# Mixture of experts: gate and up as seven half-size products in the two column halves of the array

## What is computed

```python
def route_set(hs):
    aff = jax.nn.softmax((hs @ w_router + b_router).astype(jnp.float32), axis=-1)
    gate, idx = lax.top_k(aff.T, cap)
    xe = hs[idx]
    hid = jax.nn.silu(jnp.einsum('ecd,edf->ecf', xe, w_gate)) * jnp.einsum('ecd,edf->ecf', xe, w_up)
    ye = jnp.einsum('ecf,efd->ecd', hid, w_down) * gate[..., None].astype(hid.dtype)
    return jnp.zeros(hs.shape, ye.dtype).at[idx.reshape(-1)].add(ye.reshape(-1, hs.shape[-1]))
```

## Time and profile before

| | |
|---|---|
| median of 3 runs | 4300.24 us (4299.25 to 4301.16) |
| profiled execution: span | 4305.1 us |
| PE busy | 3853.5 us, 90% of the span |
| DVE, ACT, POOL busy | 1393.0, 844.8, 419.3 us |
| bytes by DMA | 612.73 MB, mean 142 GB/s |
| experts of layer 0, layer 1 | from 1427 to 2324 us, from 3594 to 4296 us |

### The profile page before, as it was taken

How to read it: one execution, slowest core, us unless ns; L and a number is a source line. 1 busy time by engine, 2 the same in 40 slices (tenths; PEclk the granted TensorE clock), 3 DMA queues, 4 the chain that set the end, 5 groups by cost and what they waited for, 6 DMA issues and landing times. The chain is left out here.

```text
span 4305.1 us, 59887 instructions
## 1 busy us (share of the span) xinstructions
PE 3853.5 (90%) x25486; PEld 2161.3 (50%) x25486; DVE 1393.0 (32%) x2991; ACT 844.8 (20%) x1952; POOL 419.3 (10%) x675
## 2 busy tenths in 40 slices
PE   6899999677897799999997899998697886999998
PEld 4565445476644344444443655444486542444444
DVE  2452112687634200000002453113778443101010
ACT  3342010544311000000002342011534210000000
POOL 1100000221200000000001100000232100000000
PEclk9999999788998899999998899999698997999999
DMA  6201110200174666666663001110100328888884
GB/s 230 108 1 30 56 52 1 76 13 18 65 280 192 239 250 245 244 248 249 245 239 113 24 6 30 58 45 28 58 10 12 114 91 313 304 322 303 322 302 157
DMA packets 190041, 612.73 MB, mean 142 GB/s; under 512 B 34473, under 2 KB 42921, under 8 KB 183121
## 3 DMA queue, kind: packets, MB, share of 16 engines
q1 hardware_dynamic: 169232, 542.30, 33.6%
q0 software_dynamic: 20544, 66.60, 5.2%
HBM read 561.07 MB, written 47.79 MB: 141 GB/s over the span
## 5 line engine op out<-in xcount | busy, mean ns | idle before, releaser
L2534 PE MATMUL ps<-moe_w,e_hT 128*128 128x512 f32 x1024 | 445.9, 593 | 6.1 <-ACT e_hT L2578 6.1
L2497 PE MATMUL ps<-moe_w,e_xT 128*128 128x512 f32 x1024 | 450.5, 598 | 0.8 <-ACT e_xT L2559 0.8
L2504 PE MATMUL ps<-moe_w,e_xT 128*128 128x512 f32 x1024 | 444.7, 592 | 0.0
L529 PE MATMUL ps<-hT,p_w 128*128 128x512 f32 (+1 forms) x880 | 327.1, 534 | 0.0
L2497 PEld LDWEIGHTS ps<-moe_w,e_xT 128*128 128x128 f32 x1024 | 194.7, 192 | 246.7 <-issue 245.5
L2504 PEld LDWEIGHTS ps<-moe_w,e_xT 128*128 128x128 f32 x1024 | 194.6, 190 | 244.9 <-issue 244.9
L2600 DVE TENSOR_TENSOR e_hid<-e_hid,ps 128x512 f32<-128x512 f32 x64 | 43.9, 687 | 837.9 <-PE ps L2504 837.9
L2534 PEld LDWEIGHTS ps<-moe_w,e_hT 128*128 128x128 f32 x1024 | 192.0, 190 | 239.0 <-issue 239.0
L2181 PE MATMUL ps<-M,yT 128*128 128x512 f32 x576 | 259.8, 606 | 11.1 <-DMA o_br<-in_b_router_dram 7.6
L529 PEld LDWEIGHTS ps<-hT,p_w 128*128 128x128 f32 x880 | 167.2, 190 | 159.3 <-issue 153.1
L1021 PE MATMUL ps<-M 96*128 96x512 f32 (+1 forms) x400 | 183.2, 544 | 2.9 <-PEq L727 2.1
(11 more groups left out here) (356 smaller groups left out, 5507.2 us busy)
## 6 DMA issues: line engine op xcount, KB each, us to landing
moe_w<-in_w_gate_dram SPq DMA_DIRECT2D x64, 2048.0 KB, 13.2
moe_w<-in_w_up_dram SPq DMA_DIRECT2D x64, 2048.0 KB, 10.7
moe_w<-in_w_down_dram SPq DMA_DIRECT2D x64, 2048.0 KB, 17.0
o_mod_w<-in_w_ada_dram SPq DMA_DIRECT2D x24, 1024.0 KB, 10.9
m_mod_w<-in_w_ada_dram SPq DMA_DIRECT2D x16, 1024.0 KB, 5.8
p_w<-in_w_in_dram SPq DMA_DIRECT2D x6, 2048.0 KB, 7.9
r_z<-z_rows SPq DMA_DIRECT2D x20, 512.0 KB, 3.3
z_rows<-p_zo POOLq DMA_DIRECT2D x36, 256.0 KB, 2.3
```

What stands on the lines that cost most here:

```text
L529: ins = nc.tensor.matmul(ps[:, j % NB, 0:tw], w[n % RW][:, k, m * P:(m + 1) * P], hT[:, k, t0:t0 + tw], start=(k == 0), stop=(k == KT - 1))
L2497: ins = nc.tensor.matmul(ps[:, c, :], xT[:, 4 * half + k], wp[:, k, c * 512:(c + 1) * 512], start=(half == 0 and k == 0), stop=(half == 1 ...
L2504: ins = nc.tensor.matmul(ps[:, 2 + c, :], xT[:, 4 * half + k], wp[:, k, c * 512:(c + 1) * 512], start=(half == 0 and k == 0), stop=(half = ...
L2534: ins = nc.tensor.matmul(ps[:, 6 + c, :], hT2[:, 4 * half + k], wp[:, k, c * 512:(c + 1) * 512], start=(half == 0 and k == 0), stop=(half ...
```

## The change

Gate and up, seen as two matrices, are each a product of 128 tokens by 1024 by 1024. Both are cut in two along tokens, contraction and columns, and the eight block products are replaced by seven products of sums and differences of blocks (Winograd's form of Strassen's scheme). One product is 64 tokens by 512 by 512 for gate and for up at once: gate in array columns 0 to 63 (PSUM partitions 0 to 63) and up in columns 64 to 127, `ps[HF * q:HF * q + HF, b]`, 16 recorded matmuls of 64 stationary columns. DVE now forms four token sums (128 by 256 elements) and eight weight sums (128 by 2048 elements) an expert, the latter in place in the weight slots or in `t2`. ACT copies the growing sum in bank A three times an expert (`partial`), DVE joins four outputs from it (`joined`), and since up's outputs land in the other partitions, ACT moves them across after silu. Two of an expert's products, P1 and P2, and the context's products now stand ahead of the down products of the expert before, and the weights come in quarters: 1 MB (runs of 2 KB) in a ring of 16 slots.

```diff
-MOE_RW = 8
-MOE_PARTS = [(e, m, half) for e in range(NE) for m in range(3) for half in range(2)]
+MOE_RW = 16
+MOE_ORDER = [("g11", 0), ("u11", 0), ("g21", 0), ("u21", 0), ("g12", 0), ("u12", 0), ("g22", 0), ("u22", 0),
+             ("d0", -1), ("d1", -1), ("d2", -1), ("d3", -1)]
+MOE_PARTS = [(name, e + d) for e in range(NE + 1) for name, d in MOE_ORDER if 0 <= e + d < NE]
...
+    sp.dma_start(g.moe_w[:, j % MOE_RW], src[:, 4 * half:4 * half + 4, 512 * c:512 * c + 512]).then_inc(*g.sg(f"w_slot{j % MOE_RW}").up(16))
...
+    A_, B_, C_, D_, CB, CD, YB = 0, 1, 2, 3, 4, 5, 6
+    P1, P2, P6, P5, P7, P4, P3 = range(1, 8)
...
                 for j in range(RW, len(MOE_PARTS)):
+                    name, eo = MOE_PARTS[j - RW]
+                    if name[0] == "d":
+                        if need_ctx:
+                            sp.wait_ge(*dmc.at(eo + 1))
+                        else:
+                            sp.wait_ge(*dm.at(4 * eo + int(name[1]) + 1))
                     else:
+                        sp.wait_ge(*product_at(eo, {"11": P5, "12": P7, "21": P4, "22": P3}[name[1:]]))
                     load_expert_part(sp, g, I, l, j)
...
+                def product(b, x, weights, first):
+                    for k in range(4):
+                        for q in range(2):
+                            ins = nc.tensor.matmul(ps[HF * q:HF * q + HF, b, :], x[:, k], weights[q][:, k], start=(first and k == 0), stop=(k == 3),
+                                                   skip_group_check=True)
+                    ins.then_inc(*pm.up())
...
+                def first_products(e):
+                    pe.wait_ge(*xte.at(2 * e + 1))
+                    if e:
+                        pe.wait_ge(*tcd.at(3 * e))
+                    product(A_, tokens(e, 0, 0), raw(e, "11"), True)
+                    pe.wait_ge(*xte.at(2 * e + 2))
+                    if e:
+                        pe.wait_ge(*joined_at(e - 1, C11))
+                    product(B_, tokens(e, 1, 0), raw(e, "21"), True)
...
+                def other_products(e):
+                    more = e + 1 < NE
+                    pe.wait_ge(*tcd.at(3 * e + 1))
+                    pe.wait_ge(*xsd.at(4 * e + S2 + 1))
+                    pe.wait_ge(*td.at(8 * e + 4))
+                    product(A_, xs[:, S2], [t2[:, 0], t2[:, 1]], False)
+                    if more:
+                        x_transposes(e + 1, 0)
+                    if e:
+                        pe.wait_ge(*he.at(2 * e))
+                    product(D_, xs[:, S1], summed(e, "11"), True)
+                    if more:
+                        x_transposes(e + 1, 1)
+                        if need_ctx:
+                            c_transposes(e + 1)
+                    pe.wait_ge(*tcd.at(3 * e + 2))
+                    pe.wait_ge(*xsd.at(4 * e + S3 + 1))
+                    pe.wait_ge(*td.at(8 * e + 6))
+                    product(A_, xs[:, S3], summed(e, "12"), False)
+                    if more:
+                        pe.wait_ge(*xte.at(2 * e + 4))
+                    pe.wait_ge(*td.at(8 * e + 8))
+                    product(C_, tokens(e, 1, 1), summed(e, "21"), True)
+                    pe.wait_ge(*joined_at(e, C22))
+                    pe.wait_ge(*xsd.at(4 * e + S4 + 1))
+                    product(D_, xs[:, S4], summed(e, "22"), False)
...
                 for e in range(NE):
+                    other_products(e)
+                    if e + 1 < NE:
+                        first_products(e + 1)
+                        if need_ctx:
+                            context_products(e + 1)
                     for k in range(KT):
                         if k % 4 == 0:
                             pe.wait_ge(*hd.at(2 * e + 1 + k // 4))
...
             @block.scalar
+                    partial(e, P6, 1)
+                    if more:
+                        x_copy(e + 1, 0)
+                        x_copy(e + 1, 1)
+                        if need_ctx:
+                            c_copy(e + 1)
+                    partial(e, P7, 0)
+                    gate(e, C11)
+                    link(gate(e, C22))
+                    link(gate(e, C21))
+                    nc.scalar.copy(out_of(C21)[0:HF], out_of(C11)[HF:P]).then_inc(*hs.up())
+                    gate(e, C12)
+                    nc.scalar.copy(out_of(C22)[0:HF], out_of(C12)[HF:P]).then_inc(*hs.up())
+                    if more:
+                        partial(e + 1, P1, 0)
+                        if need_ctx:
+                            context_copy(e + 1)
+                    for half in range(2):
+                        act.wait_ge(*htr.at(2 * e + half + 1))
+                        nc.scalar.copy(hT2[:, 4 * half:4 * half + 4].rearrange("p k n -> p (k n)"), ps[:, C_ + half]).then_inc(*he.up())
...
             @block.vector
+                def weight_sums(e, i):
+                    if i == 0:
+                        dve.wait_ge(*product_at(e, P2))
+                        if need_ctx:
+                            dve.wait_ge(*cgu.at(e + 1))
...
+                        to, a, b = ((b11, b12, b11), (t2[:, q], b22, b11), (b12, b22, b12), (b21, t2[:, q], b21))[i]
+                        nc.vector.tensor_tensor(to, a, b, ALU.subtract).then_inc(*td.up())
...
+                token_sums(0)
+                for i in range(4):
+                    weight_sums(0, i)
...
+                    joined(e, C22)
+                    joined(e, C21)
+                    hidden(e, 0)
+                    joined(e, C12)
+                    hidden(e, 1)
+                    if more:
+                        token_sums(e + 1)
+                        for i in range(3):
+                            weight_sums(e + 1, i)
+                    dve.wait_ge(*dm.at(4 * e + 4))
...
+                    if more:
+                        weight_sums(e + 1, 3)
```

More of the change, by code:

```diff
@@ L2468, in _, with x_transposes @@
             def _(pe):
[L2469 to L2478, removed]
+                def x_transposes(e, half):
+                    if half == 0:
+                        pe.wait_ge(*ga[e % 2].at(16 * (e // 2 + 1)))
+                        if e >= 2:
+                            pe.wait_ge(*he.at(2 * (e - 2) + 1))
+                    else:
+                        pe.wait_ge(*xte.at(2 * e + 1))
+                    for k in range(4):
+                        ins = nc.tensor.transpose(ps[:, C_, k * P:(k + 1) * P], xe[:, e % 2, (4 * half + k) * P:(4 * half + k + 1) * P], g.ident)
@@ new lines, in context_products @@
+                def context_products(e):
+                    pe.wait_ge(*xtec.at(e + 1))
+                    if e:
+                        pe.wait_ge(*chd.at(e))
+                    for half in range(2):
+                        parts = [raw(e, f"{half + 1}1"), raw(e, f"{half + 1}2")]
+                        for k in range(4):
+                            for q in range(4):
+                                ins = nc.tensor.matmul(ps[32 * q:32 * q + 32, CB, :], xTc[:, 4 * half + k], parts[q % 2][q // 2][:, k],
+                                                       start=(half == 0 and k == 0), stop=(half == 1 and k == 3))
+                    ins.then_inc(*cgu.up())
@@ L2488, in _ @@
+                x_transposes(0, 0)
+                x_transposes(0, 1)
                 if need_ctx:
                     c_transposes(0)
+                first_products(0)
+                if need_ctx:
+                    context_products(0)
+                    context_turned(0)
                 for e in range(NE):
[L2491 to L2495, removed]
-                            for k in range(4):
-                                ins = nc.tensor.matmul(ps[:, c, :], xT[:, 4 * half + k], wp[:, k, c * 512:(c + 1) * 512],
-                                                       start=(half == 0 and k == 0), stop=(half == 1 and k == 3))
-                        ins.then_inc(*gm.up())
@@ new lines, in partial, with gate @@
+                def partial(e, p, i):
+                    act.wait_ge(*product_at(e, p))
+                    if p == P1 and e:
+                        act.wait_ge(*joined_at(e - 1, C21))
+                    if p == P6 and e:
+                        act.wait_ge(*joined_at(e - 1, C12))
+                    if p == P7:
+                        act.wait_ge(*joined_at(e, C11))
+                    nc.scalar.copy(part[:, i], ps[:, A_]).then_inc(*tcd.up())
+                def gate(e, c):
+                    act.wait_ge(*joined_at(e, c))
+                    r, n = (0, 0) if c == C11 else (0, 1) if c == C12 else (1, 0) if c == C21 else (1, 1)
+                    return nc.scalar.activation(hid[HF * r:HF * r + HF, 512 * n:512 * n + 512], out_of(c)[0:HF], ACT.Silu)
@@ new lines, in context_copy, with context_gate @@
+                def context_copy(e):
+                    act.wait_ge(*cgu.at(e + 1))
+                    nc.scalar.copy(gu[:], ps[:, CB]).then_inc(*cev.up())
+                def context_gate(e):
```

(5 more changed lines are left out.)

267 lines of the change are left out of this document (146 added, 121 removed).

## The result

The changed kernel takes 4250.7 us (median of 4 runs, 4248.7 to 4252.8), the kernel before 4299.7 us beside it: ratio 0.9884, 95% interval 0.987 to 0.990, or 49 us less. The forecast was 4236, so 15 us of the gain did not come. Of all executions told here three took far longer (7559 us of the kernel before, 8097 of it with runs of 2 KB, 6340 of the one with its transposes in one group), and no ratio counts them.

The account below looks back on a forecast made before the run. PE's products were taken to bound both layers, with weight transfer close behind in layer 1. Gains of 91.2 us less 26.5 lost at first and last experts gave 64.7, from 4300.2 to 4236 us, range 4222 to 4268.

Parts of the forecast that it names:

- The product: PE, gate and up: paired 64-column matmuls share the array, 3.43 us each, seven making 24.03 for 27.46, −3.43 us an expert.
- The rival of imperfect sharing: Every pair of narrow matmuls: halves share imperfectly, a product takes 4.39 us, 215 us more in all, 4451; chance 0.07.
- The switches: PE changing between wide and narrow matmuls: 0.12 us each, +0.72 us an expert in layer 1, +0.60 in layer 0.
- The bounds of the sum: Range for PE's changes between wide and narrow: 0.08 or 0.20 us each, +8 or −16 us over 32 experts.
- The floors: Time of an expert after the change: 40.86 us in layer 1 and 52.68 us in layer 0.
- The hidden values: Wait before down for hidden transposes and copy: zero net in layer 1; in layer 0 +0.50 and −0.66 us.
- The sums: DVE's weight sums: 2.29 us each, covered in middle experts with 5 us or more to spare, uncovered at a layer's ends.
- The first expert's gap: After P2 in each layer's first expert PE waits for four weight sums: 9.4 us in layer 1, 8.9 in layer 0.
- the cold clock: PE's clock falls in the wait of each layer's first expert: 1.8 us more each time.
- The tail: Each layer's last expert, before down: no next expert's products cover the hidden values, 3.7 us for 1.4, +2.3 each time.
- The weights: Quarter loads arrive in time: 2.6 us each, 1.5 to land, d0 at 24.4 us, down due at 26.9, no cost.
- the first rival: Layer 1's weight transfer becomes the bound: down waits 2 us in each expert, 32 us lost, 4268; chance 0.12.

Follow-up runs that it names:

- small sums: Changed kernel with each weight sum cut from 2048 to 128 elements a partition, results not the reference's; ratio 0.9823 to the kernel before.
- another beginning: Changed kernel with another order of products and weight sums in each layer's first expert alone; ratio 0.9845 to the kernel before, median 4231.8 us.

## Why the prediction was right, and where it fell short

**The product: right.** 3.43 us was predicted and measured, and the run with up's matmuls left out shows that the second half is free. The rival of imperfect sharing is refuted. One of its grounds was misread: a pair needs two weight loads, not four (161 loads in the 40.94 us expert, 112 of them for 56 pairs). The Trainium skill, page "TensorE: Matmul & The Clock Gate", section "Measured speedup vs the span model", gives 2.38 for three column tiles; two tiles of 64 columns show no such loss here, with 0.429 us a pair, and the measurement decides.

**The switches: right in sum.** 0.12 each was predicted; the rows show 0.15 more for each of three narrow groups between wide ones and 0.15 more for each of two groups of token transposes, 0.75 us an expert in layer 1 for the 0.72, and grouping the transposes gave 0.30. (The bounds of the sum, +8 and −16 us, are worked out with six switches in both layers; with the five more of layer 0 they are +7 and −14.) The floors came out 0.08 and 0.05 us above the forecast, 2 us in all.

**The hidden values: right.** In the middle 0.28 us of wait, inside the floor.

**The sums: right.** 2.29 us, and covered in the middle. The first expert's gap was 9.1 and 7.8 us for 9.4 and 8.9. The chain of layer 1's first expert after the change, from its first token transposes to P6 behind the gap, and the window at P6's start:

```profile
3552.84 1.13 PE ps L2517 x4
...
3563.78 2.35 DVE moe_w L2745 x2
...
3570.39 2.30 DVE e_t L2745
...
3572.83 6.27 PE ps L2533 x16
```

```profile
3572.83:3576.50 3.67, 3.67 (x10) 1.31 (x12) 3.67 (x2) 0.00 (x0) 0.00 (x0) 0.50 0.00 0
```

P6 took 6.27 us for 3.58, so the cold clock cost 2.7 for the 1.8 predicted (layer 0: 54.47 − 52.73 = 1.7). The window has a granted clock of 0.50, the 1.2 GHz level. The tail came to 3.4 us for 3.7, from P3's end, at 4218.38, to down:

```profile
4218.41 0.70 DVE e_cb L2751
...
4221.16 0.66 PE ps L2617 x4
4221.82 3.44 PE ps L2628 x8
```

**The weights: the step that failed.** The prediction said of d0 "That is no cost, with a cover of 2.5 us at d0". Its loads were released where the step had them (g22 at 15.4 us for 15.1). What failed are two small sizes that ate the cover: a quarter at the plateau takes 2.7 us (1.05 MB at 387 GB/s with several under way) for 2.6, times three for g22, u22 and d0, and the time around them was 3.7 us (d0's landing at 3684.56 less g22's issue at 3672.78 are 11.8, less 8.1) for the 1.5 allowed. That is 2.5 us, so d0 landed in the expert shown as down fell due or just behind, and in nine of 14 down waited, 12.3 us in all. The share was off too: 0.91 was predicted from the 33.1 us that the queue took with runs of 4 KB, and the 34.5 of 2 KB runs made it 0.96 to 0.97. The size of the step is 11.4 us of period in this profile and 16 in the timed runs of the order that takes it away. It is the first rival's mechanism at a third of its price (32 us): not the transfer's rate, since 0.97 of share is enough, but the place of one load in a strict queue. The clock is part of it: the worst wait was 2.3 us and that expert 3.65 longer, at a granted 0.96.

**Left out of the sum:** the first gather, queued behind the last loads in 2 KB runs, comes 2 us later (PE waits 10.0 for 8.0 in layer 1, 11.1 for 9.3 in layer 0): 3.8 us. That 2 KB runs do it is shown by the kernel before with such runs: 9.7 and 11.3.

These make up the difference: 4235.5 + 11.4 (down quarters) + 3.8 (gathers) + 2 (floors) + 0.8 (clock) − 1.7 (gaps, tail) = 4251.8, measured 4250.7. The two profiled spans differ by 58.8 us, 10 more than the medians, and those 10 lie outside the expert stages (9 of them between the two), where both kernels do the same. Inside the stages, from the last matmul of `stage_topk` on, the profiles differ by 49.3 us.

**Open:** how long down waits with one and the same order of loads. The changed kernel's profile has 12.3 us, with small sums it is 3.6, with another beginning 5.2, with less of up 5.4. The small sums come with a shorter scatter on POOL (1.58 us), but the two others have the long one (3.38) and wait little more, so neither the sums nor the scatter alone explain the 12.3. There is one profile of each, and with a cover this thin the waits may differ from one execution to the next; no run here settles it. What is shown is that the order of the loads removes the waits.

## What to carry to other kernels

When a change brings an engine's time within a tenth of the transfer's, a share of busy time says nothing on lateness any more: write for each load when it is released, what is queued ahead of it, and when it is due, allow for the latency of a queue that starts empty (3.7 us here, beside 2.7 for each 1 MB load), and give the queue's place to what is due first, separately for each stage that needs another order. Test a reordering for what it releases: the transposes in one group, 0.3 us better on PE, lost 16 us through a slot that came free one product later. A stationary operand of 64 columns was no loss here, with another half-width matmul beside it: the pair took the 0.429 us of one full-width matmul.

## What was not expected of the hardware

POOL's indirect scatter takes 3.38 us beside weight sums on DVE, and 1.58 without them. In the changed kernel's timelines of POOL and DVE it starts under the last two sums:

```profile
3700.27 3.38 POOL L2495 DMA_INDIRECT out_dram<-e_ye,all_tok  x1 [36.31 <-DVE e_ye L2785]
```

```profile
3699.91 4.48 DVE L2745 TENSOR_TENSOR moe_w<-e_t,moe_w 128x2048 f32<-128x2048 f32 x2
```

POOL began at 3700.27 and was done at 3703.65, DVE's two sums ran from 3699.91 to 3704.39. The Trainium skill, page "GPSIMD Engine Reference", section "Specifications", says that POOL's SBUF interfaces are shared with VectorE and contended by DVE instructions with two SBUF inputs; the trace agrees in so far as a scatter takes 1.8 us longer beside such instructions. And after a wait of 2.1 us the next matmuls ran at a lower granted clock (32 context matmuls in 5.34 us for 3.64, at 0.68), and late loads of 2.3 and 3.9 us made their experts 3.65 and 6.2 us longer.
